# A branch over the loop of spilled blocks that falls through, and the first expert pair's buffers given back by quarters

## The reference, cut to what matters

```python
def hier_moe(h, w_grp, w_exp, w1, w3, w2):
    # per token: best of 4 groups, then the best 2 of its 8 experts (32 experts in all)
    ...
    # for each expert e, over the tokens that chose it (1024 choices in all):
    #   y = (silu(x @ w1[e]) * (x @ w3[e])) @ w2[e]     w1, w3: 1024 x 512, w2: 512 x 1024
    # each token adds its two y, each times its gate

x = x + hier_moe(rmsnorm(x), ...)
h = rmsnorm(x)
x = x + sigmoid(h @ w_pg) * (p @ w_ple)
return rmsnorm(x)
```

## Time and profile before

| what | value |
|---|---|
| median of 3 executions | 1804.99 us |
| the profiled execution's own time | 1810.17 us |
| its span | 1808.4 us |
| mean granted TensorE clock | 0.985 of full |
| TensorE matmul busy | 1678.5 us (93%) |
| VectorE, ScalarE busy | 805.5 us (45%), 548.5 us (30%) |
| read from memory | 346.03 MB |

### The profile page before, as it was taken

The page is one execution under the profiler, slowest core; times in us unless marked ns, Lnnn a source line. Parts: engine busy times, 40 slices in busy tenths (PEclk is TensorE's granted clock), DMA queues, the critical chain, the costliest instruction groups (busy, mean ns, idle before and its releaser), DMA issues. The chain is left out here.

```text
span 1808.4 us, 19972 instructions
## 1 busy us (share of the span) xinstructions
PE 1678.5 (93%) x8083; PEld 1163.9 (64%) x8083; DVE 805.5 (45%) x1247; ACT 548.5 (30%) x913; POOL 50.2 (3%) x89
## 2 busy tenths in 40 slices
PE   2999999889989999999999999998999898989878
PEld 2788756568868888888788876765344343434346
DVE  4783567664633222365622463245233232323245
ACT  4322367643362222232532450523100000000036
POOL 0000010100000000000000000000200000000000
PEclk9999999999999999999999999999999999999989
DMA  9784210011622222221422021257899999999941
GB/s 347 238 323 146 94 70 1 2 70 57 247 69 94 93 94 93 105 71 47 163 93 94 2 92 47 97 225 292 328 429 428 430 430 430 430 430 430 428 175 47
DMA packets 89879, 351.75 MB, mean 195 GB/s; under 512 B 9958, under 2 KB 42386, under 8 KB 73657
## 3 DMA queue, kind: packets, MB, share of 16 engines
q1 hardware_dynamic: 87226, 346.08, 48.6%
q0 software_dynamic: 2560, 4.37, 0.7%
HBM read 346.03 MB, written 8.43 MB: 196 GB/s over the span
## 5 line engine op out<-in xcount | busy, mean ns | idle before, releaser
L574 DVE TENSOR_TENSOR arena<-ring,arena 128x1024 fp32r<-128x1024 f32 x120 | 146.9, 1225 | 230.2 <-ACT arena L636 207.1
L2889 PE MATMUL ex_h<-ring,u_big_tail 128*64 128x512 f32 x512 | 154.0, 611 | 15.0 <-DMA ring<-in_w 8.1
L579 PE MATMUL up_ps<-h_high,arena 128*128 128x512 f32 x352 | 137.6, 391 | 3.3 <-DVE arena L574 3.3
L580 PE MATMUL up_ps<-arena 128*128 128x512 f32 x352 | 137.0, 389 | 0.0
L581 PE MATMUL up_ps<-h_high,arena 128*128 128x512 f32 x352 | 137.0, 389 | 0.0
L636 ACT CAST arena<-ring 128x1024 fp32r<-128x1024 f32 x81 | 84.8, 1047 | 149.7 <-PE up_ps L581 81.2
L2889 PE MATMUL ex_h<-s_ab,u_big_tail 128*64 128x512 f32 x272 | 114.4, 596 | 1.5 <-DVE u_big_tail L2860 1.5
L2889 PEld LDWEIGHTS ex_h<-ring,u_big_tail 128*64 128x64 f32 x512 | 47.6, 139 | 80.0 <-issue 79.1
L2860 DVE TENSOR_TENSOR u_big_tail<-ex_x,vcol 128x512 f32<-128x512 f32 x32 | 20.6, 686 | 175.4 <-PE ex_x L2853 175.4
L3167 ACT ACTIVATE u_big_tail<-ex_h 128x512 f32<-128x512 f32 x16 | 9.6, 598 | 293.5 <-PE ex_h L2889 293.5
L579 PEld LDWEIGHTS up_ps<-h_high,arena 128*128 128x128 f32 x352 | 66.1, 188 | 18.8 <-DVE arena L574 3.6
(11 more groups left out here) (597 smaller groups left out, 3637.0 us busy)
## 6 DMA issues: line engine op xcount, KB each, us to landing
ring<-in_w SPq DMA_DIRECT2D x42, 2048.0 KB, 32.3
s_ab<-in_w SPq DMA_DIRECT2D x32, 2048.0 KB, 31.8
ring<-in_w_in SPq DMA_DIRECT2D x18, 2048.0 KB, 8.2
ring<-in_w_ada SPq DMA_DIRECT2D x24, 1024.0 KB, 7.0
reg_a<-in_w SPq DMA_DIRECT2D x10, 2048.0 KB, 31.8
w1flat<-in_w SPq DMA_DIRECT2D x10, 2048.0 KB, 32.9
ring<-in_w_ffn_gate SPq DMA_DIRECT2D x11, 1024.0 KB, 5.2
ring<-in_w_ffn_up SPq DMA_DIRECT2D x11, 1024.0 KB, 7.5
```

The lines of the kernel that those rows point to most:

```text
L574: return engine.tensor_tensor(lo, v, hi.bitcast(F32), ALU.subtract)
L579: nc.tensor.matmul(ps, x[0], y[0], start=start, stop=False)
L580: nc.tensor.matmul(ps, x[0], y[1], start=False, stop=False)
L2889: mm = nc.tensor.matmul(ps[half, :], xT[:, k, half], ws[j][:, k, cols], start=(k == 0), stop=(k == k_end - 1))
```

## The change

Two things change. First, `load_piece` loads a quarter of a matrix (2 of its 8 row groups). Matrices 9 to 12, the second filling of buffers 0 to 3, are loaded in four pieces each. The first pair's two products give each quarter back as it has been read, by the semaphores `eaten[0]` and `eaten[1]`, and by `h1` and `h3` for the last one. `turn(1)` moves from ahead of the first pair's x·w3 into its middle. `wait_expert` counts three more increments of 16 for these buffers from the second filling on. Second, what TensorE does after the loop of spilled blocks becomes a function `way_out`, which is emitted twice: once in the body of `If(n < 1)`, and once behind the loop in its `Else`. The other engines keep `each`.

```diff
+REFILL = 4
+
+def load_piece(b, sp, m, g):
+    n = len(b.wbuf)
+    view, dram = expert_matrix(b, m)
+    k = view.shape[1] // REFILL
+    sp.dma_start(view[:, g * k:(g + 1) * k, :], dram[:, g * k:(g + 1) * k, :]).then_inc(b.wfull[m % n], 16)
+
 def wait_expert(b, eng, m):
-    eng.wait_ge(b.wfull[m % len(b.wbuf)], 16 * (m // len(b.wbuf) + 1))
+    i, turn = m % len(b.wbuf), m // len(b.wbuf)
+    extra = REFILL - 1 if turn and i < 4 else 0
+    eng.wait_ge(b.wfull[i], 16 * (turn + 1 + extra))
...
             load_expert(b, sp, 8)
-            for m in range(len(b.wbuf), 6 * PAIRS):
+            for i in range(2):
+                for g in range(REFILL):
+                    if g < REFILL - 1:
+                        sp.wait_ge(eaten[i], g + 1)
+                    else:
+                        sp.wait_ge((h1, h3)[i], 1)
+                    for j in range(2):
+                        load_piece(b, sp, len(b.wbuf) + 2 * i + j, g)
+            for m in range(len(b.wbuf) + 4, 6 * PAIRS):
...
+            def first_pair(ps, i, g):
+                mm = pair(ps, 0, i, range(g * KD // REFILL, (g + 1) * KD // REFILL), slice(0, CH))
+                return mm.then_inc(eaten[i], 1) if g < REFILL - 1 else mm.then_inc((h1, h3)[i], 1)
...
             turn(0)
-            for s in range(PAIRS + 1):
+            pe.wait_ge(xt, 1)
+            for g in range(REFILL):
+                first_pair(ps_h1, 0, g)
+            pe.wait_ge(b.ple_out, 2 * NT)
+            for g in range(REFILL):
+                if g == REFILL // 2:
+                    turn(1)
+                first_pair(ps_h3, 1, g)
+            for s in range(1, PAIRS + 1):
...
-            spill.tensor(pe, n_spill)
-            for g in range(2):
+            def way_out():
+                for g in range(2):
...
+                fin.tensor(pe, lambda t: pe.wait_ge(added, HOME * LAST + (3, 4, 6, 8)[t]))
+
+            spill.tensor(pe, n_spill, way_out)
...
+    def before(self, eng, n, body, rest):
+        with eng.If(n < 1):
+            rest()
+        with eng.Else():
+            with eng.Fori(0, n) as j:
+                body(j)
+            rest()
...
-        self.each(pe, n, body)
+        self.before(pe, n, body, rest)
```

More of the change, by code:

```diff
@@ L2938, in stage_experts @@
     w2_rest = [b.sem(f"ex_w2rest{j}") for j in range(2)]
+    eaten = [b.sem(f"ex_eaten{i}") for i in range(2)]
     LAST = PAIRS - 1
@@ L3045, in _ @@
                     pe.wait_ge(xt, s + 1)
-                    if s:
-                        pe.wait_ge(silu, s)
+                    pe.wait_ge(silu, s)
                     pair(ps_h1, s, 0, range(KD // 2), slice(0, CH))
[L3049 to L3055, removed]
+                pe.wait_ge(hm, s)
+                if s >= 2:
+                    pe.wait_ge(added, HOME * (s - 2) + 1)
+                for f in range(KE):
+                    mm = nc.tensor.transpose(ps_t[:, f * P:(f + 1) * P], b.hm[:, f::KE], b.ident[:])
+                mm.then_inc(h_turned, 1)
                 if s < PAIRS:
@@ L3059, in _ @@
                     pe.wait_ge(added, HOME * (s - 1))
-                if s:
-                    pe.wait_ge(hmt, s)
-                if 0 < s < PAIRS:
+                pe.wait_ge(hmt, s)
+                if s < PAIRS:
                     for h in range(2):
@@ L3068, in _ @@
                 if s < PAIRS:
-                    if s == 0:
-                        pe.wait_ge(b.ple_out, 2 * NT)
                     pair(ps_h3, s, 1, range(KD), slice(0, CH)).then_inc(h3, 1)
-                if 0 < s < PAIRS:
                     back(s - 1)
-            spill.tensor(pe, n_spill)
-            for g in range(2):
[L3076 to L3080, removed]
-                    if g:
[L3082 to L3089, removed]
+            def way_out():
+                for g in range(2):
+                    if g:
+                        for j in range(2):
+                            pe.wait_ge(w2_rest[j], 16)
+                    for h in range(2):
+                        mm = pair(ps_y[h], LAST, 2, range(g * KE // 2, (g + 1) * KE // 2), slice(h * CH, (h + 1) * CH))
+                        if g:
+                            mm.then_inc(y_last, 1)
+                pe.wait_ge(picked, PAIRS)
+                for i, bank in last_home:
+                    pe.wait_ge(low_last, i % 2 + 1)
+                    if bank is ps_y[0]:
+                        pe.wait_ge(low_last, 2)
+                    send_home(nc, b, bank, i).then_inc(home, 1)
+                fin.tensor(pe, lambda t: pe.wait_ge(added, HOME * LAST + (3, 4, 6, 8)[t]))
+            spill.tensor(pe, n_spill, way_out)
         @block.vector
@@ L3228, in pool, with tensor @@
         self.each(pool, n, body)
-    def tensor(self, pe, n):
+    def tensor(self, pe, n, rest):
         b, nc = self.b, self.nc
```

## The result

| | kernel before | changed kernel |
|---|---|---|
| median, 13 runs each | 1809.62 us (1803.97 to 1817.52) | 1799.93 us (1796.12 to 1804.93) |
| ratio of times | | 0.9942, 95% interval 0.9931 to 0.9953 |
| profiled execution, its span | 1810.17, 1808.4 us | 1800.41, 1798.6 us |

The change is worth 0.58%, 10.5 us of 1809.6. Forecast were 12.3 us and a time of 1792.7 us in a range of 1788.5 to 1799.0. The direction and the two places were right; the time lies 0.9 us outside the range.

What follows compares the result with a forecast made beforehand. The prediction took the stream of expert weights to bound the loop, and a chain through TensorE the end. Terms 6.2 + 3.0 + 3.1 = 12.3 us off 1804.99 gave 1792.7 us, range 1788.5 to 1799.0.

Steps and rivals of the forecast that it cites:

- The stop: TensorE's 6.51 us of issue at the branch over the spilled-block loop, taken as a far target's fetch; 6.2 us go.
- The Trainium skill's rule of the prediction: Instructions are prefetched in sequence in 16 KB blocks; a taken branch outside what is held waits for its block.
- The clock: Product behind the branch pays 10.09 instead of 7.10 us at a clock of 0.50 after idleness; 3.0 us go.
- A fall that stays: Low end of the gain on the product behind the branch: the clock still falls, gain 0.
- The long jump: TensorE's jump over the loop and second copy of `way_out` after its last matmul; hidden by the last stores, cost 0.
- The quarters: Returning quarters of the first pair's matrices early fills the weight queue's gap at 1281.5 to 1285.5 us; 3.1 us.
- Idle worth: 4.0 × (1 - 93/429) = 3.1 us: Queue gap from 1281.5 to 1285.5 us, at 93 GB/s against 429 when full, counted as 3.1 us of idleness.
- from there on the queue doesn't run dry: Once the ninth load ends, pieces already wait, so the weight queue stays filled; part of the 3.1 us.
- the lead reaches it whole: The 3.1 us head start lasts to the expert loop's end, near 1723 us, where TensorE waits for weights.
- the gather of rows and the scatters take the room: Rival in the weight queue: the 3.1 us lead is lost, or a later gap swallows it; 1795.8 us, chance 0.09.
- the rival in which each pays its own start and end: Rival on the weight queue: pieces don't overlap, 12 more at 1.5 us, 18 us; 1813.8 us, chance 0.04.
- the terms don't depend on that, so 1804.99 - 12.3: Final sum: 12.3 us taken from the shown runs' median, 5.2 us below the profiled execution, giving 1792.7 us.

Runs made afterwards that it cites:

- the short body: Kernel before, branch still taken, with seven of the eight steps of a spilled block's first two products left out of the loop's body; ratio to before 0.9955.
- the fall-through: Kernel before with only the way out placed directly behind the compare; whole loads, transposes where they were; ratio to before 0.9960.

## Why the prediction was wrong

**The stop, 6.2 us: right.** Idle time 8.34 to 2.21 us, which is 6.1. The mechanism, a fetch of a target that is too far, is shown by the short body (0.69 us of issue with the branch still taken, and no instruction block in that time). The block of 16 KB stands in the trace of before from 1734.10 to 1735.02 us, between the copy's end (1730.16) and the product (1736.67). The Trainium skill's rule of the prediction ("Runtime: NRT & Kernel Launch", section "Instruction fetch mechanics") agrees with both traces: a block where the far branch is taken, none where the target is near.

**The clock, 3.0 us: right in the profile** (10.08 to 7.09 us), but not each time: 8.8 us once among eleven. "A fall that stays" was one end of that term, and it occurred. Timed, the fall-through gave 7.2 us with an interval that holds the forecast's 9.2.

**The long jump, 0: right.** Its fetch is in the trace, behind the last matmul, and the distance to the span's end is unchanged.

**The quarters, 3.1 us: the step that was mis-sized.** The prediction put it thus: "Idle worth: 4.0 × (1 - 93/429) = 3.1 us" and "from there on the queue doesn't run dry". The second came true, and the lead was 3.5 us, 12 us behind the first pair's start. The first is mis-sized: it takes all that the gap didn't move for idleness. Without the scatters the same gap shows 2.2 us of idleness. The rest, some 1 us, was time that the eight scatters (issued by GpSimd from 1279.9 us on) took from the loads. The row could have warned: the DMA share was 0.56 while 93 GB/s is 0.22 of the full queue's 429, so much of what was missing was slowness and not idleness. Filling the gap doesn't give it back; it moved to the next 10 us. So "the lead reaches it whole" failed too: of 3.5 us, 12 us behind the first pair's start, 2.2 are left on the mean of four profiles, and 1.1 in the first profile of the changed kernel. With the scatters out of the loop the quarters are worth 2.0 us, the same within what the profiles tell. I had a rival, "the gather of rows and the scatters take the room", at 0.09, with the whole 3.1 us lost. Why single profiles differ by 2.1 us stays open. The pieces themselves ran at 386 to 420 GB/s, so nothing of the 18 us came of the rival in which each pays its own start and end.

**The gain in all.** 12.3 us forecast, 10.5 measured; 9.1 us of the profiles' 9.8 us between the spans are the stop and the clock.

**The time: the base.** 1792.7 us forecast, 1799.93 measured, 7.2 us apart. Of these, 4.6 are the base: the median of before was 1804.99 us over three runs and is 1809.62 over thirteen, and 1811.4 to 1811.8 in the three later comparisons. 1.8 are the gain's shortfall, and the remaining 0.8 is between the ratio of times and the difference of the medians. The step that failed is "the terms don't depend on that, so 1804.99 - 12.3": the terms don't, but the sum does. I had seen that the profiled execution lay 5.2 us above the median and that one of the three runs lay 4.6 above it (1809.62), and gave the base no room in the range. The range had a slip as well: the ends of the terms give 1804.99 - 13.9 = 1791.1 to 1804.99 - 5.9 = 1799.1 us, not "1789 to 1796"; the measured time is outside that too. Against the profiled execution's own time the same terms gave 1797.9, 2.0 us below the measured median.

## What to carry to other kernels

Where a branch is nearly always taken over a long body, put the usual way directly behind the compare, and let the long jump fall where another engine's work is still to come; look for idle time of "issue" with an instruction block in it, and for a cold clock behind it. When a gap in a full queue is to be filled, don't take all the missing bytes for idleness. Where the DMA share is well above the share of the bytes (0.56 against 0.22 here), transfers run slowly there, and what small ones cost inside the gap isn't given back by closing it. Those that only a rare case needs belong in that case's branch. A forecast of a time needs the spread of the base, not only that of the change.

## What the runs showed that was not expected

- Eight scatters of 128 rows of 8 bytes each cost the weight queue about as much as 0.8 to 1.05 MB of weights: 2.4 to 2.5 us in the windows beside a full queue, 1.8 to 2.0 us in the mean streams. Beside them, packets of 4 KB took 204 ns instead of 159.
- The stream varies by 2.1 us between executions with the same loads in the same places (436.4 to 438.5 us with quarters and scatters), and by 1.0 us between the two with quarters and without scatters (435.1 and 436.1). So the scatters aren't all of it. Why was not found.
- Much of the spread between executions goes with the clock. The changed kernel's 13 runs have mean granted clocks of 0.981 to 0.990, and the lower the clock the longer the time (correlation -0.81, 0.8 us for each 0.001); that the clock is the cause wasn't tested. All twelve later profiles have a stretch of 10 to 14 us at 0.50 near 360 us, which the two first ones (before and changed) don't have, and their first pair starts between 1276.6 and 1279.6 us instead of at 1275.5 and 1276.0.
